# Router products over scaled token chunks on four column groups, and the last modulation part moved into the gates

## What is computed

```python
mod = jax.nn.silu(cond) @ w_mod + b_mod            # six parts of 2048, for the latent and the context condition
sh1, sc1, gt1, sh2, sc2, gt2 = jnp.split(mod, N_MOD, axis=-1)
...
merged = jax.nn.sigmoid(gate_a) * (o_gla @ w_branch_a) + jax.nn.sigmoid(gate_b) * (o_swa @ w_branch_b)
x = x + gt1 * (merged @ w_out)
h2 = rmsnorm(x, g_norm2) * (1 + sc2) + sh2
aff = jax.nn.softmax((h2 @ w_router).astype(jnp.float32), axis=-1)      # 16 experts
gate, idx = lax.top_k(aff.T, cap)                                       # 64 latent + 16 context tokens each
xs = h2[idx]
hid = jax.nn.silu(xs @ w_gate[e]) * (xs @ w_up[e]);  ye = (hid @ w_down[e]) * gate
x = x + gt2 * (ye added at idx)
```

## Time and profile before

| | us |
|---|---|
| median of 3 runs (lowest, highest) | 2985.03 (2980.07, 2987.07) |
| profiled execution, whole | 2982.53 |
| span of its trace, first to last instruction | 2980.7 |
| PE busy in the span | 2837.4 |
| DVE busy | 2062.2 |
| ACT busy | 1607.4 |
| POOL busy | 281.0 |

### The profile page before, as it was taken

The page is one execution under the profiler, slowest core; times in us unless marked ns, Lnnn a source line. Parts: engine busy times, 40 slices in busy tenths (PEclk is TensorE's granted clock), DMA queues, the critical chain, the costliest instruction groups (busy, mean ns, idle before and its releaser), DMA issues.

```text
span 2980.7 us, 38357 instructions
## 1 busy us (share of the span) xinstructions
PE 2837.4 (95%) x13981; PEld 2100.4 (70%) x13981; DVE 2062.2 (69%) x2384; ACT 1607.4 (54%) x1943; POOL 281.0 (9%) x182
## 2 busy tenths in 40 slices
PE   6899899999999999999999987999999999999993
PEld 4798548899668888888888873666666666666662
DVE  2436655544866766677655556888888888888884
ACT  4345324444854444444343434777777777777773
POOL 0000010000000000000010000111221122111111
PEclk9999999999999999999999998999999999999996
DMA  9822342221023333433362279999999999999994
GB/s 373 291 71 71 123 167 85 76 75 57 1 73 128 132 140 113 157 128 113 137 259 71 84 287 364 401 403 400 383 382 381 389 388 386 378 387 389 388 393 163
DMA packets 160779, 684.72 MB, mean 230 GB/s; under 512 B 13940, under 2 KB 14020, under 8 KB 99004
## 3 DMA queue, kind: packets, MB, share of 16 engines
q1 hardware_dynamic: 147216, 613.45, 53.4%
q0 software_dynamic: 11408, 69.78, 7.4%
q10 hardware_dynamic: 2064, 0.26, 0.1%
HBM read 651.91 MB, written 31.60 MB: 229 GB/s over the span
## 4 chain that ended last, share of the span: by engine, by line
PE 91%; DVE 4%; ACT 2%; DMA 1%; issue 1%; POOL 0%; DVEq 0%; POOLq 0%; ACTq 0%; SPq 0%
PE ps L855 38%; PE ps L1319 24%; PE ps L1346 12%; PE ps L874 5%; PE ps L881 3%; PE ps L1292 1%; PE ps L1146 1%; PE ps L1157 1%; PE ps L819 1%; PE ps L1024 1%; PE ps L1128 1%; PE ps L1256 1%; PE ps L989 1%; DVE ar L1835 0%; PE ps L801 0%
## 5 line engine op out<-in xcount | busy, mean ns | idle before, releaser
L855 PE MATMUL ps<-split_weights,split_tokens 128*128 128x512 f32 x5040 | 1159.0, 391 | 4.4 <-issue 2.9
L855 PEld LDWEIGHTS ps<-split_weights,split_tokens 128*128 128x128 f32 x5040 | 945.2, 188 | 212.8 <-issue 11.5
L1319 PE MATMUL ps<-split_experts,split_xsT 128*80 128x512 f32 x3072 | 709.3, 392 | 4.9 <-DVE split_experts L2074 4.9
L480 DVE TENSOR_TENSOR split_weights<-ring,split_weights 128x512 fp32r<-128x512 f32 x384 | 266.4, 694 | 540.7 <-ACT split_tokens L477 538.6
L476 ACT ACTIVATE split_weights<-ring 128x512 fp32r<-128x512 f32 x384 | 242.7, 632 | 736.8 <-PE ps L855 611.7
L1319 PEld LDWEIGHTS ps<-split_experts,split_xsT 128*80 128x80 f32 x3072 | 454.9, 148 | 257.4 <-DVE split_experts L2074 5.8
L2074 DVE TENSOR_TENSOR split_experts<-hT,split_experts 128x2048 fp32r<-128x2048 f32 x240 | 548.0, 2289 | 75.6 <-ACT split_experts L1657 75.4
L1657 ACT ACTIVATE split_experts<-hT 128x2048 fp32r<-128x2048 f32 x240 | 460.7, 1920 | 153.2 <-PE ps L1319 111.8
L1346 PE MATMUL ps<-split_experts,split_hidT 128*80 128x512 f32 x1536 | 361.0, 394 | 0.0
L1346 PEld LDWEIGHTS ps<-split_experts,split_hidT 128*80 128x80 f32 x1536 | 225.5, 148 | 121.9
L483 DVE TENSOR_TENSOR split_tokens<-hT,split_tokens 128x640 fp32r<-128x640 f32 x304 | 250.5, 824 | 0.0
(11 more groups left out here) (261 smaller groups left out, 1929.0 us busy)
## 6 DMA issues: line engine op xcount, KB each, us to landing
ring<-w_mod SPq DMA_DIRECT2D x96, 1024.0 KB, 5.3
hT<-w_exp_gate SPq DMA_DIRECT2D x80, 1024.0 KB, 7.2
hT<-w_exp_up SPq DMA_DIRECT2D x80, 1024.0 KB, 7.1
hT<-w_exp_down SPq DMA_DIRECT2D x80, 1024.0 KB, 9.5
ring<-w_in SPq DMA_DIRECT2D x64, 1024.0 KB, 5.2
ring<-w_exp_gate SPq DMA_DIRECT2D x32, 1024.0 KB, 8.0
ring<-w_exp_up SPq DMA_DIRECT2D x32, 1024.0 KB, 10.3
ring<-w_exp_down SPq DMA_DIRECT2D x32, 1024.0 KB, 7.6
```

Of the source, the lines that this page charges most:

```text
L480: a = self.eng.tensor_tensor(spW[:, s, 1, :], raw, spW[:, s, 0, :].bitcast(F32), ALU.subtract)
L855: mm = pe.matmul(ps[:, b, :], spX[:, s, x, b * P:(b + 1) * P], spW[:, s, w, :], start=(k == 0 and x == w), stop=(k == n_k - 1 and x == 1))
L1319: mm = pe.matmul(ps[0:CAP, bank + i, :], xsT[:, x, k, :], spE[:, s, w, col:col + BANK], start=(k == 0 and x == w), stop=(k == KT - 1 and x ...
```

## The change

1. Modulation part 5 is formed on VectorE in the gates as well: 48 instead of 32 rows of multiply-adds a turn, spread by the table `MOD_ROWS` over pieces 3 to 23 and 27 to 47 (three of each 21 carry two rows). The 16 `mod_granules` behind the projection and their loads are gone. Each `mod_sum` on TensorE is now four matmuls of 256 columns into the four column groups, three times a turn, at other pieces.
2. x1 is no longer normalised before the router. In the turns 1 to 3 of the projection ScalarE squares the chunk n-1 (`square`), and after piece 8 VectorE multiplies that chunk in place with the folded scale (`scale_x1`); GpSimd stores the chunk first and loads the scale by chunks.
3. Behind the projection TensorE transposes the scaled tokens by chunks of 512 columns, and multiplies four k blocks at once in four column groups (`logits`). The shift goes through as two further columns. The four partial sums are added by a matmul with `group_sum`; the root r and the shift are applied to the logits on VectorE. The rows h2 = x1 * r + B2 are formed beside that, for the gather.
4. Seven granules of the first expert are loaded ahead (two at the projection's end, five after the logits), its first three pieces are split before the gathered rows are there, the last round of each top 8 leaves out its replacement, VectorE writes the first gather index, and the slots `exp_slot` are in another order.

The core of the diff (declarations, address changes and what only follows from them are left out):

```diff
+MOD_ROWS = [[r for r in range(48) if 3 + 24 * (r // 24) + r % 24 * 21 // 24 == k] for k in range(48)]
...
+                for r in MOD_ROWS[first + k]:
+                    m, kk = r // 4, r % 4
+                    part, row, g = m // 4, r % KT, G_GATE + mod_place(m)
+                    v = ring[:, g % SLOTS, kk * BANK:(kk + 1) * BANK]
+                    if kk == 0:
+                        dve.wait_ge(slot_ready[g % SLOTS], n * 96 + 16 * (g // SLOTS + 1))
...
+            sync.wait_ge(n2_h, 2 * NT)
+            sync.wait_ge(lg_pe, 1)
+            for j in range(2, 7):
+                expert(0, j)
+            sync.wait_ge(xs_ld, 16)
...
+            def scale2_chunk(n):
+
+                if n >= 2:
+                    pool.wait_ge(x1_sc, NT * (n - 1))
+                for who in range(2):
+                    at = 4 * D + n * BANK
+                    pool.dma_start(A2c[n % 2][:, who, :], row_bcast(mod_dram[who, at:at + BANK])).then_inc(a2_ld[n % 2], 16)
+
+            def store_x1(n):
+
+                pool.wait_ge(wo_ev, NT * (n + 1))
+                cols = slice(n * BANK, (n + 1) * BANK)
+                pool.dma_start(y_dram.rearrange("(t p) d -> p t d", p=P)[:, :, cols], x1[:, :, cols]).then_inc(x1_st, 16)
...
+            def mod_sum(n, part, bank_copied=None):
+
+                pe.wait_ge(z_rd, n * 96 + (2 * GH + 1 + 32 * (part + 1)))
...
+                for i in range(4):
+                    cols = slice(i % 2 * 2 * P, (i % 2 + 1) * 2 * P)
+                    mm = pe.matmul(ps[32 * i:32 * i + 32, 7, 0:2 * P], mod_ones, mod_acc[2 * part + i // 2][:, cols],
                                    start=True, stop=True)
...
+            pe.wait_ge(sq_part, 3 * NT)
+            pe.wait_ge(br_ld, 16)
+            for k in range(KT):
+                mm = pe.transpose(ps[:, 7, 2 * k:2 * k + 2], arows[0:2, k * P:(k + 1) * P], ident[0:2, 0:2])
+            mm.then_inc(n2_tr, 1)
+
+            def x1_transposes(c, t):
+
+                i = NT * c + t
+                pe.wait_ge(x1_sc, i + 1)
...
+                for j in range(4):
+                    v = x1[:, t, (4 * c + j) * P:(4 * c + j + 1) * P] if c < 3 else xa3[:, t, j * P:(j + 1) * P]
+                    mm = pe.transpose(ps[:, bank, j * P:(j + 1) * P], v, ident)
+                mm.then_inc(n2_tr, 1)
+
+            def logits(c):
...
+                pe.wait_ge(n2_cp, NT * (c + 1) + 1)
+                for bank, lo, hi in ((0, 0, LAT), (1, LAT, TOK + 2)):
+                    for g in range(4):
+                        mm = pe.matmul(ps[32 * g:32 * g + 32, bank, 0:hi - lo], wrt[:, 4 * c + g, :], x1T[c][:, g, lo:hi],
+                                       start=(c == 0), stop=(c == 3), skip_group_check=True)
...
+            chunk_transposes(0)
+            chunk_transposes(1)
+            logits(0)
+            chunk_transposes(2)
+            logits(1)
+            chunk_transposes(3)
+            logits(2)
+            logits(3)
...
-            with act.Fori(1, 3) as n:
-                out_pieces(sp, act, n, AHEAD, KT)
-                out_pieces(sp, act, n + 1, 0, AHEAD)
-
+            def square(n, t, junk):
+
+                act.wait_ge(wo_ev, NT * n + t + 1)
+                act.activation(junk, x1[:, t, n * BANK:(n + 1) * BANK], ACT.Square,
+                               accum_out=part[:, n, t:t + 1]).then_inc(sq_part, 1)
+                act.wait_ge(sq_part, NT * n + t + 1)
+
+            for n in range(1, 4):
+                for t in range(NT):
+                    out_pieces(sp, act, n, AHEAD + 2 * t, AHEAD + 2 * t + 2)
+                    square(n - 1, t, ps[:, 5, :])
+                out_pieces(sp, act, n, AHEAD + 2 * NT, KT)
+                if n < 3:
+                    out_pieces(sp, act, n + 1, 0, AHEAD)
...
+            def copy_x1T(c):
+
+                for t in range(NT):
+                    i = NT * c + t
+                    act.wait_ge(n2_tr, i + 2)
+                    act.activation(x1T[c][:, :, t * P:(t + 1) * P],
+                                   ps[:, X1_BANKS[i % 6], :].rearrange("p (k t) -> p k t", k=4), ACT.Copy).then_inc(n2_cp, 1)
...
+            copy_x1T(0)
+            copy_x1T(1)
+            act.wait_ge(mc_st, 64 + 32 * 12)
             for t in range(NT):
...
+                square(3, t, modc[:, :])
+            act.wait_ge(n2_sq, 1)
+            act.activation(stat[:, NT:2 * NT], stat[:, 0:NT], ACT.Sqrt, scale=1.0 / D, bias=epsb[:, :]).then_inc(n2_sq, 1)
+            copy_x1T(2)
+            copy_x1T(3)
...
+            split_expert(0, 0, AHEAD)
             act.wait_ge(xs_tr, 1)
...
+            for n in range(4):
+                if n:
+                    out_pieces(sp, dve, n, AHEAD, 9)
+                    dve.wait_ge(x1_st, 16 * n)
+                    dve.wait_ge(sq_part, NT * n)
+                    dve.wait_ge(a2_ld[(n - 1) % 2], 32 * ((n - 1) // 2 + 1))
+                    for b in range(NT):
+                        scale_x1(n - 1, b)
+                    out_pieces(sp, dve, n, 9, KT)
+                else:
+                    out_pieces(sp, dve, n, AHEAD, KT)
...
                 for b in range(NT):
                     dve.wait_ge(wo_rd, n * NT + (NT + b + 1))
...
+                    xv = x1[:, b, n * BANK:(n + 1) * BANK]
                     dve.tensor_tensor(xv, xv, wtmp[:, b, :], ALU.add).then_inc(wo_ev, 1)
...
+                    if n == 3:
+                        dve.wait_ge(wo_ev, n * NT + b + 1)
+                        scale_x1(n, b)
+            dve.wait_ge(sq_part, 4 * NT)
+            dve.tensor_reduce(stat[:, 0:NT], part[:, :, 0:NT].rearrange("p c t -> p t c"), AX.X, ALU.add).then_inc(n2_sq, 1)
+            dve.wait_ge(n2_sq, 2)
+            r = stat[:, NT:2 * NT]
+            ch.step(dve.reciprocal(r, r))
+            dve.wait_ge(ab_ld, 32)
             for t in range(NT):
...
+                dve.wait_ge(n2_tr, 3 * NT + t + 2)
+                for v, cols in ((x1[:, t, 0:3 * BANK], slice(0, 3 * BANK)), (xa3[:, t, :], slice(3 * BANK, D))):
+                    dve.scalar_tensor_tensor(v, v, r[:, t:t + 1], B2[:, who, cols], ALU.mult, ALU.add).then_inc(n2_h, 1)
...
+            lg = ps[:, 2, 0:NT * NE].rearrange("p (t e) -> p t e", t=NT)
+            ch.step(dve.tensor_tensor(a0, lg, r.unsqueeze(2).to_broadcast([P, NT, NE]), ALU.mult))
```

371 lines of the change are left out of this document (167 added, 204 removed).

## The result

The changed kernel takes 2990.62 us (median of 12 runs, 2987.72 to 2993.63), the kernel before 2984.86 in the same comparison (12 runs, 2980.07 to 2991.11): a ratio of 1.0019, 95% interval 1.0011 to 1.0027. The forecast was 2986.9. The profiled execution took 2990.93 us (span 2989.1), 8.4 us more than the profiled one before (2982.53).

The account below looks back on a forecast made before the run. TensorE was taken as the bound, busy 2837.4 of 2980.7 us, with a chain through all engines before the first expert. -1.2 + 25.8 - 22.7 = +1.9 us gave 2984.4 against the profiled execution, 2986.9 against the median; range 2975 to 2998.

Parts of the forecast that it names:

- gates, sums on TensorE: Gates: twelve new half-width modulation sums at 0.55 us replace eight at 0.98, -1.2 us.
- three stalls: Projection: TensorE stands 6.5 us in each of three turns, as VectorE's piece 9 waits for the fifth square, +19.5 us.
- what the stalls do to the products behind: Projection: TensorE's clock falls to half behind each stall, 2.1 us lost each time, +6.3 us.
- T0: The end of the last projection product, 1748.2 in the profile before; the first expert started 83.9 us later.
- T0 to the first step on the logits: Behind the projection: the shorter chain up to the work on the logits gains 17.5 us.
- from there to the gather's issue: Logits to first gather: three more small steps at 0.28 us each, against 1.0 gained in top 8 and 0.6 at the index.
- gather, issue to TensorE: First gather: its 5.9 us from issue to TensorE's first transpose stay as they were, 0 change.
- gathered rows to first expert: Before the first expert: 5.4 us go, since three pieces are already split during the top 8.
- Rival D: Gates: VectorE falls behind with its double rows, +11 us, 2998; chance 6%.
- Rival A: Projection: the wait does not bite, VectorE is let through before TensorE runs dry, 2961; chance 5%.
- Rival B: Projection: stalls come but the clock stays up after them, and the gather is quick, 2977.5; chance 17%.
- Rival C: Behind the projection: TensorE at half clock before the tenth copy, ScalarE's copies slowed to the transposes' pace, +7.6, 2994.5; chance 16%.

Follow-up runs that it names:

- e1: The changed kernel with VectorE scaling x1 ahead of piece 13 instead of piece 9 in the projection: 2966.39 us.
- e4: e1 and e3 together, on the changed kernel: 2961.87 us.
- e7: e5 with the fifth row of h2 made behind the softmax instead of ahead of it: 2958.78 us.
- e9: The changed kernel with ScalarE squaring x1 behind each piece from piece 3 on, instead of every second one: 2965.67 us.
- e2: The changed kernel with VectorE scaling x1 ahead of piece 10 instead of piece 9 in the projection: 2978.11 us.
- e5: e4 with the semaphore for VectorE's three splits raised by a small GpSimd memset behind the gather, not by GpSimd's queue: 2958.0 us.
- e3: The changed kernel with VectorE's first three first-expert splits waiting for a semaphore from GpSimd's queue behind the first gather: 2989.34 us.

## Why the prediction was right, and where it was off

The forecast's picture held and the time came out 3.7 us above it. Some of that closeness is luck: the sum was worked out from the profiled execution, and profile against profile it is 6.5 us short. By its own steps, in the two profiled executions:

| step | predicted | measured |
|---|---|---|
| start to the first gate product | 0 | -0.4 |
| gates, sums on TensorE | -1.2 | -0.3, with the row below |
| gates, VectorE's double rows | 0 | no wait |
| three stalls | +19.5 | +19.6 |
| what the stalls do to the products behind | +6.3 | +7.5 |
| T0 to the first step on the logits | -17.5 | -18.5 |
| from there to the gather's issue | -0.8 | +0.4 |
| gather, issue to TensorE | 0 | **+5.4** |
| gathered rows to first expert | -5.4 | -5.3 |
| lower clock, taken off | +1.0 | in the rows above |
| first expert to the end | 0 | +0.1 |

But for rounding, the measured column adds up to the 8.4 us between the two spans.

**Gates.** From the first gate product to T0 the kernel before took 895.8 us, and the kernels without stalls (e1, e4 to e7, e9) 894.7 to 895.7; the kernel after, less its 27.1 us of stalls, 895.5. So the gain is 0.1 to 1.1 us, and 1.2 was predicted. The sums themselves were sized rightly: one now costs 0.57 us (925.68 to the next product at 926.25) where 0.55 was taken, and 12 x 0.57 - 8 x 0.98 = -1.0. TensorE waited for nobody between 853 and 1555, so VectorE's 83 us of extra work stopped nothing. Rival D falls.

```profile
925.68 0.64 PE L1214 MATMUL ps<-cst 128*32 128x256 f32 x8
```

**Stalls.** Length, number, place and releaser are as written (6.5 us, three, VectorE's split of piece 9), and e1, e2 and e9 show the circle behind them. Rival A falls. The clock's share was taken as 6.3 us and is 6.7 to 7.1; the rest of the 7.5, at the ends and starts of the rows of products, wasn't thought of. Rival B falls for a stall of 6.5 us (the clock fell behind three of three), though not for one of 3.15 (one of three).

**T0 to the first expert.** ScalarE's ten copies took 5.01 us, as predicted from 0.51 each. Rival C falls because its condition didn't come about: the clock stayed at full until behind the tenth copy, and ten groups of four transposes took 4.58 us (1775.61 on), 0.46 each, less than a copy. It fell later, to 0.50 in 1788 to 1791, and there four groups took 3.33 us, 0.83 each, more than a copy; by then ScalarE was behind and waited for none of them. So whether slow transposes would have cost what rival C says is not shown.

```profile
1776.30 5.01 ACT L1677 ACTIVATE ar<-ps 128x512 f32<-128x512 f32 x10 [0.20 <-PE ps L1282]
...
1786.51 0.30 ACT L1686 ACTIVATE stat<-stat,epsb 128x5 f32<-128x5 f32 x1
```

```profile
1779.00:1782.00 3.00, 3.00 (x33) 2.03 (x32) 2.89 (x5) 2.97 (x8) 0.47 (x1) 1.00 0.00 0
...
1788.00:1791.00 3.00, 3.00 (x17) 2.57 (x20) 3.00 (x3) 3.00 (x7) 1.10 (x2) 0.50 0.05 18
```

The root and its reciprocal were there 12.5 us behind T0 (13.5 predicted), the rows of h2 24.6 (25.5). From the logits to the gather 0.8 was to be gained and 0.4 was lost: the affinities' transposes ran at half clock (1.23 us; 0.71 before), and from VectorE's last step on the indices (L2118) to the gather's row lie 1.6 us, no less than before with the copy (1.4), though 0.6 was to be saved there.

**The step that failed** is one sentence: "Its 5.9 us from 1815.40 to TensorE's 1821.31 stay." They didn't, since the change also moved three splits of VectorE into just that stretch. The prediction has them made "during the top 8". ScalarE's halves are (1813.0 to 1818.5), but VectorE makes the top 8 itself, so its halves can only come behind the indices, from 1822.79 on, where the gather runs. The prediction counted this move as a pure gain (5.4 us of splits out of the chain) and asked only whether the splits were ready in time, not what they run beside. The gain came, 5.3 us, and the gather took back 5.4. Of the two halves of this trade e5 keeps the one and undoes the other: its stretch from T0 to the first expert is 60.1 us, where 61.2 had been predicted and 65.9 came. The earlier trace rows showed the gather's price beside an idle VectorE only. The warning stood in the trace of before, in rows that the prediction doesn't use: in the expert loop the same instruction takes 2.57 us beside such splits, and its scatter 7.17.

```profile
1886.40 2.57 POOL L728 DMA_INDIRECT ar<-h_rows,gidx  x1 [0.83 <-POOL gidx L725]
...
1907.21 7.17 POOL L755 DMA_INDIRECT y_rows<-ar,sidx  x1 [16.84 <-DVE ar L2102]
```

**The sum.** Profile against profile the change costs 8.4 us, where +1.9 was worked out; the gather's 5.4 and 1.1 from all other rows together make the difference. Median against median it is 5.8, since the profiled execution before lay 2.3 us under its median and the one after 0.3 above. The range of 2975 to 2998 held, but it was drawn from rivals that didn't come; the cause of the miss wasn't among them.

So the change is worth having once its two side effects are gone: 2958.0 us against 2984.6, 26.6 us or 0.9% under the kernel before, by one line's place, one semaphore and a small memset.

## What to carry to other kernels

When one engine is made to wait for another, write down what that other engine has queued ahead, and what each of those waits for; if the list comes back to the first one's customer, there is a stall of fixed length (here split, square, five scalings, split: 6.5 us) that moving either end by a few pieces removes. When work is moved off the critical path into a gap, ask what else runs in that gap, as an engine that seems free may be held off by another's operands. A signal that an instruction is done has to come from an instruction behind it, not from its queue.

## What the runs showed of the hardware

- GpSimd's indirect gather of 80 rows takes 0.98 us with VectorE idle and 0.97 beside a tensor_tensor with one input in PSUM (one run), but 6.78 beside three tensor_tensor of 128x2048 whose inputs both lie in SBUF, until 0.8 us after their end. The Trainium skill (SBUF — State Buffer, section "Who interferes with whom") says that a VectorE instruction with two SBUF inputs contends with a GpSimd instruction that reads SBUF and that one with at most one SBUF input, outside the two-port modes, doesn't; these rows agree. Its further inference, that a tensor_tensor leaves the generation of descriptors alone, is no warrant for this gather, which reads its row numbers from SBUF; direct stores, at 0.53 to 0.56 us beside rows with two SBUF inputs, agree with it. How long the hold lasts varied: 2.96 us when the splits began 0.2 us ahead of the row, 2.44 between two of them. What decides that stays open.
- TensorE's clock was at half (1.2 of 2.4 GHz) for some 3 to 6 us behind each of three stalls of 6.54 us, and stayed at full behind two of three stalls of 3.15 us. With products in the stall it stayed at full.
- A semaphore that GpSimd's queue raises behind an indirect DMA let VectorE start 0.2 us before the row of that DMA began (e3, e4).
